# A hybrid encoder layer on one core: the first rows normalised and turned by halves, two feature tiles instead of one as plain products, splits and loads started at other places, and 32 small products of ones at the start

## The reference

```python
x = x + 0.5 * (silu(rms(x) @ w_gate1) * (rms(x) @ w_up1)) @ w_down1      # width 2816
P = rms(x) @ w_in                                                        # 7 x 512 columns
aq, ak, av, hq, hf, hi, hg = split(P)
A = chunked attention, 8 heads x 64, rms on q and k, 9 chunks of 64 keys, bias by distance
B = gated linear recurrence, 4 heads x 128, f = lb + (1 - lb) * sigmoid(hf), rms and silu gate
x = x + concat(A, B) @ w_out
x = x + 0.5 * (silu(rms(x) @ w_gate2) * (rms(x) @ w_up2)) @ w_down2
```

## Time and profile before

| | us |
|---|---|
| median of 3 runs | 1974.71 (1974.49 to 1977.51) |
| the profiled execution, its own time | 1979.15 |
| its span, first to last instruction | 1977.6 |
| PE busy in the span | 1897.7 (96%) |
| DVE, ACT, POOL busy | 1116.0, 676.9, 440.3 |
| mean granted clock of PE | 0.984 |

### The profile page before, as it was taken

The page is one execution under the profiler, slowest core; times in us unless marked ns, Lnnn a source line. Parts: engine busy times, 40 slices in busy tenths (PEclk is TensorE's granted clock), DMA queues, the critical chain, the costliest instruction groups (busy, mean ns, idle before and its releaser), DMA issues.

```text
span 1977.6 us, 24542 instructions
## 1 busy us (share of the span) xinstructions
PE 1897.7 (96%) x9296; PEld 1570.5 (79%) x9296; DVE 1116.0 (56%) x1503; ACT 676.9 (34%) x1023; POOL 440.3 (22%) x350
## 2 busy tenths in 40 slices
PE   6899999999999999999998789989999999999998
PEld 5788888887888888888887567777888888878887
DVE  6866666665555630244545664348666666655564
ACT  7333333323333432211122563244333223323332
POOL 3322422431111100011223420001422422321030
PEclk9999999999999999999998999999999999999999
DMA  5454444537755343321342410114354444468663
GB/s 163 144 183 148 159 169 146 175 135 283 247 193 195 107 155 112 117 96 64 127 142 90 144 57 1 64 64 149 139 179 146 165 162 152 149 226 284 216 195 132
DMA packets 209004, 295.50 MB, mean 149 GB/s; under 512 B 14512, under 2 KB 104760, under 8 KB 208896
## 3 DMA queue, kind: packets, MB, share of 16 engines
q1 hardware_dynamic: 193184, 253.28, 37.5%
q0 software_dynamic: 7360, 25.51, 4.0%
q10 hardware_dynamic: 8352, 15.27, 2.1%
HBM read 205.37 MB, written 91.25 MB: 150 GB/s over the span
## 4 chain that ended last, share of the span: by engine, by line
PE 89%; DVE 5%; issue 2%; ACT 2%; DMA 1%; POOL 1%; DVEq 0%; SPq 0%; ACTq 0%; POOLq 0%
PE ps L636 27%; PE ps L638 27%; PE ps L637 27%; PE ps L809 2%; PE ps L670 1%; PE ps L905 1%; PE ps L892 1%; PE ps L925 1%; DVE wlo L1494 1%; DVE hXlo L1465 0%; DVE xs L1447 0%; DMA tok_scratch<-y 0%; DVE hTlo L1425 0%; DMA xs<-x 0%; PE ps L800 0%
## 5 line engine op out<-in xcount | busy, mean ns | idle before, releaser
L636 PE MATMUL ps<-hThi,whi 128*128 128x512 f32 x864 | 338.7, 392 | 11.9 <-DVE wlo L1494 6.4
L637 PE MATMUL ps<-hTlo,whi 128*128 128x512 f32 x864 | 337.6, 391 | 0.0
L638 PE MATMUL ps<-hThi,wlo 128*128 128x512 f32 x864 | 337.5, 391 | 0.0
L636 PE MATMUL ps<-whi 128*128 128x512 f32 x616 | 241.7, 392 | 9.2 <-DVE wlo L1568 9.2
L638 PE MATMUL ps<-whi,wlo 128*128 128x512 f32 x616 | 241.1, 391 | 0.0
L637 PE MATMUL ps<-wlo,whi 128*128 128x512 f32 x616 | 241.1, 391 | 0.0
L636 PE MATMUL ps<-hXhi,whi 128*128 128x512 f32 x504 | 197.9, 393 | 8.8 <-DVE wlo L1494 8.8
L636 PEld LDWEIGHTS ps<-hThi,whi 128*128 128x128 f32 x864 | 163.1, 189 | 46.0 <-DVE wlo L1494 6.6
L637 PE MATMUL ps<-hXlo,whi 128*128 128x512 f32 x504 | 197.3, 391 | 0.0
L638 PE MATMUL ps<-hXhi,wlo 128*128 128x512 f32 x504 | 197.3, 391 | 0.0
L638 PEld LDWEIGHTS ps<-hThi,wlo 128*128 128x128 f32 x864 | 163.0, 189 | 34.1
(11 more groups left out here) (186 smaller groups left out, 2959.7 us busy)
## 6 DMA issues: line engine op xcount, KB each, us to landing
hid_scratch<-hid SPq DMA_DIRECT2D x132, 256.0 KB, 2.6
raw<-ffn_w_gate SPq DMA_DIRECT2D x44, 512.0 KB, 3.7
raw<-ffn_w_up SPq DMA_DIRECT2D x44, 512.0 KB, 4.9
wdb<-ffn_w_down SPq DMA_DIRECT2D x44, 512.0 KB, 4.1
wd_scratch<-wdb SPq DMA_DIRECT2D x88, 256.0 KB, 4.5
raw<-hid_scratch SPq DMA_DIRECT2D x80, 256.0 KB, 2.7
rawx<-hid_scratch SPq DMA_DIRECT2D x74, 256.0 KB, 2.7
raw<-w_in SPq DMA_DIRECT2D x28, 512.0 KB, 5.2
```

Of the source, the lines that this page charges most:

```text
L636: pe.matmul(dst, ahi, bhi, start=first, stop=False, skip_group_check=onto)
L637: pe.matmul(dst, ahi, blo, start=False, stop=False, skip_group_check=onto)
L638: return pe.matmul(dst, alo, bhi, start=False, stop=last, skip_group_check=onto)
```

## The change

- Two feature tiles are plain instead of one (`NPLAIN` = 2). The written start has 16 products instead of 15, and none of them needs `t2` or `t34`; each feed-forward has 156 products instead of 155. The first four products need only the first half of the width of the first four rows.
- The first four rows are normalised, turned, split and kept by halves of 512 columns, each half in one PSUM bank (`early_norm`, `early_turn`, `early_hi_part`, `early_lo_part`, `early_keep`); the squares of rows 4 to 7 stand on ACT behind all of that.
- PE begins with 24 products of a 128x128 tile of ones, 2 more after the second row's half and 6 after the fourth's (`idle_products`). The tile is filled by POOL, and the load of its later content waits for the first product.
- Pieces 0, 1 and 2 of each down projection are split during the last feature tile (`PIECE_AFTER`) instead of behind it.
- The loads of q, k, v and bias go from POOL's queue to SP's, bias and v of the second pair earlier; the masked corners are written once into the scratch tensor of the bias by two transfers. The first scores no longer wait for `kS`: unit 1 uses banks 6 and 7, and `read_out` of the last head stands behind units 0 and 1 on DVE.
- The second half of the output weights is loaded at the head of attention; the first gate and up weights of the second feed-forward behind rows 2 and 4 of `x_scratch`, instead of ahead of row 0. The first two weights of the second feed-forward are split ahead of the last row's square.
- The last piece of all counts each of its four tiles, so that each can be taken when it is done.

```diff
-START = [(0, 0), (0, 1), (1, 0), (0, 2), (0, 3), (1, 2), (0, 4), (0, 5), (0, 6), (0, 7),
-         (1, 4), (1, 1), (1, 3), (1, 5), (1, 6)]
-PRODUCTS = START + [(e, i) for e in range(2, FT) for i in range(NPROD)]
-WEIGHTS = [(0, 0), (0, 1), (1, 0), (0, 2), (0, 3), (1, 2), (1, 4), (1, 1), (1, 3), (1, 5), (1, 6)]\
-    + [(e, i) for e in range(2, FT) for i in range(NPROD)]
+START = [(0, 0), (0, 1), (1, 0), (1, 1), (0, 2), (0, 3), (1, 2), (1, 3),
+         (0, 4), (0, 5), (1, 4), (1, 5), (0, 6), (0, 7), (1, 6), (1, 7)]
+PRODUCTS = START + [(e, i) for e in range(NPLAIN, FT) for i in range(NPROD)]
+WEIGHTS = [(0, 0), (0, 1), (1, 0), (1, 1), (0, 2), (0, 3), (1, 2), (1, 3)]\
+    + [(e, i) for e in range(NPLAIN, FT) for i in range(NPROD)]
 SEQ = len(PRODUCTS)
...
+    if n <= 16:
         return PREPARED_AFTER.get(n, [])
-    return [n + 3] if n + 3 < NW else []
+    return [n - 1] if n - 1 < NW else []
 
...
+PIECE_AFTER = [(FT - 1, 1), (FT - 1, 3), (FT - 1, 4)]
...
+            return 6 if v == 1 else 2 * ((v + 1) % 2)
 
...
+            gate_up(0, 1, ffn1_w_gate, ffn1_w_up)
             for t in range(4, TT):
                 sp.dma_start(xs[:, t, :], x[0, t * P:(t + 1) * P, :]).then_inc(x_loaded[t], 16)
-            gate_up(0, 1, ffn1_w_gate, ffn1_w_up)
...
+            load_qk(0)
+            sp.wait_ge(bias_stored, 48)
+            sp.wait_ge(proj_done, PROJ_OUTS)
+            load_bias(0)
+            load_bias(1)
+            sp.wait_ge(qk_turned, 4)
+            load_qk(1)
+            stored(7)
+            load_v(0)
+            load_v(1)
+            out_pieces(1)
...
             for t in range(TT):
                 sp.wait_ge(x_added, TT + t + 1)
                 sp.dma_start(x_d[t * P:(t + 1) * P, :], xs[:, t, :]).then_inc(x_saved[t], 16)
+                if t in (2, 4):
+                    gate_up(1, t // 2 - 1, ffn2_w_gate, ffn2_w_up)
...
-                mm.then_inc(piece_done, 1)
...
+            def idle_products(n):
+                for _ in range(n):
+                    pe.matmul(ps[:, 0:P], gn[:, :], gn[:, :], start=True, stop=True)
+            pe.wait_ge(mhalf_set, 2)
+            idle_products(24)
             pe.wait_ge(ident_loaded, 16)
             for t in range(4):
+                early_turn(t, 0)
+                if t == 1:
+                    idle_products(2)
+            idle_products(6)
+            products(0, 0, 1)
+            early_turn(0, 1)
+            early_turn(1, 1)
+            products(0, 1, 2)
+            early_turn(2, 1)
+            early_turn(3, 1)
+            for t in range(4, TT):
+                products(0, t - 2, t - 1)
                 turn_tile(R_FFN1, t)
-            products(0, 0, 1)
-            turn_tile(R_FFN1, 4)
-            turn_tile(R_FFN1, 5)
-            products(0, 1, 2)
-            turn_tile(R_FFN1, 6)
...
 
+            def early_hi_part(t, h):
+                act.wait_ge(turned if h else early_turned, t + 1)
+                act.activation(hThi[:, 4 * h:4 * h + 4, t * P:(t + 1) * P],
+                               bank(early_bank(t)).rearrange("p (k c) -> p k c", k=4), ACT.Copy)\
+                   .then_inc(hT_hi_ready if h else early_hi, 1)
...
+            weight_hi(0, 2)
+            early_hi_part(0, 1)
+            early_hi_part(1, 1)
+            weight_hi(0, 3)
+            early_keep(0, 1)
+            early_keep(1, 1)
+            early_hi_part(2, 1)
+            early_hi_part(3, 1)
+            weight_hi(0, 4)
+            early_keep(2, 1)
+            early_keep(3, 1)
+            weight_hi(0, 5)
+            for t in range(4, TT):
                 square(R_FFN1, t)
-            keep_turned(R_FFN1, 0)
-            weight_hi(0, 0)
-            keep_turned(R_FFN1, 1)
-            keep_turned(R_FFN1, 2)
-            weight_hi(0, 1)
-            keep_turned(R_FFN1, 3)
-            square(R_FFN1, 4)
-            square(R_FFN1, 5)
-            weight_hi(0, 2)
-            square(R_FFN1, 6)
...
+            def early_norm(t, h):
+                dve.wait_ge(rstd_ready, t + 1)
+                if t == 0:
+                    dve.wait_ge(gain1_loaded, 16)
+                at = slice(h * HALF, (h + 1) * HALF)
+                dve.scalar_tensor_tensor(xs[:, t, at], xs[:, t, at], rstd[:, t:t + 1], gain[:, at],
+                                         ALU.mult, ALU.mult).then_inc(y_ready if h else early_y, 1)
+            def early_lo_part(t, h):
+                if h:
...
                 before = EVACS * F + t + 1
                 if q == 0:
...
+            weight_lo(0, 2)
+            early_lo_part(0, 1)
+            early_lo_part(1, 1)
+            weight_lo(0, 3)
+            early_lo_part(2, 1)
+            early_lo_part(3, 1)
+            for t in range(4, TT):
+                weight_lo(0, t)
                 normalise(R_FFN1, t)
-            hT_lo(R_FFN1, 0)
-            weight_lo(0, 0)
-            hT_lo(R_FFN1, 1)
-            hT_lo(R_FFN1, 2)
-            weight_lo(0, 1)
...
                             nmax[:, hd, t:t + 1])
                     last.then_inc(unit_max, 1)
+                if v == 1:
+                    read_out(HH - 1)
                 if 2 <= v < NV + 2 and not by_scalar(v - 2):
...
+                    weight_lo(1, 0)
+                    weight_lo(1, 1)
                 add(8 + t, t, 1)
...
+            pool.wait_ge(prod_done, 1)
             pool.dma_start(gn[:, :], hgrn_out_norm_g[0:1, :].to_broadcast([P, P])).then_inc(gn_loaded, 16)
...
+            pool.wait_ge(bias_stored, 16)
+            corner = masked.unsqueeze(1).to_broadcast([CHUNK, AH, CHUNK])
+            pool.dma_start(bias_d[:, CHUNK:P, 0:CHUNK].rearrange("h t s -> t h s"), corner)\
+                .then_inc(bias_stored, 16)
+            pool.dma_start(bias_d[:, 0:CHUNK, BAND - CHUNK:BAND].rearrange("h t s -> t h s"), corner)\
+                .then_inc(bias_stored, 16)
```

More of the change, by code:

```diff
@@ L266, in build @@
                 hXlo = keep("hXlo", [P, 12, HALF], F32R, c2)
-                gu_q = keep("gu_q", [P, HALF], where=c2)
+                gu_q = keep("gu_q", [P, NPLAIN, HALF], where=c2)
             with ExitStack() as c2:
@@ L435, in build @@
         av_loaded = [sem(f"av_loaded{p}") for p in range(2)]
-        bias_loaded = sem("bias_loaded")
-        bias_masked = sem("bias_masked")
+        bias_loaded = [sem(f"bias_loaded{p}") for p in range(2)]
         qk_sq = sem("qk_sq")
@@ L612, in _, with out_pieces, stored, load_qk @@
             wo = w_out[0].rearrange("(q k p) c -> q p k c", p=P, k=2)
[L613 removed]
+            def out_pieces(h):
                 for q in range(4):
                     piece(P_OUT + 4 * h + q, 0, wo[q][:, :, h * HALF:(h + 1) * HALF], 2)
[L616 to L617 removed]
+            def stored(n):
+                for s in range(2):
+                    sp.wait_ge(proj_stored[s], 64 * n)
+            def load_qk(p):
+                for w in range(2):
+                    sp.dma_start((qin, kin)[w], tok[:, 2 + w, p * P:(p + 1) * P]
+                                 .rearrange("(t p) c -> p t c", p=P)).then_inc(qk_loaded[w], 16)
+            def load_bias(p):
+                sp.dma_start(bias[:, p % 2, :, :], bias_d[2 * p:2 * p + 2].rearrange("h t s -> t h s"))\
+                  .then_inc(bias_loaded[p % 2], 16)
+            def load_v(p):
+                sp.dma_start(vin[:, p % 2, :, :], tok[:, 4, p * P:(p + 1) * P]
+                             .rearrange("(t p) c -> p t c", p=P)).then_inc(av_loaded[p % 2], 16)
+            out_pieces(0)
+            stored(6)
+            sp.wait_ge(y_ready, 2 * TT)
+            sp.wait_ge(turned, 2 * TT)
+            load_qk(0)
[9 more added lines that the diff above has]
+            out_pieces(1)
+            for p in range(2, PAIRS):
+                sp.wait_ge(qk_turned, 4 * p)
+                load_qk(p)
+                sp.wait_ge(unit_out, NU * (p - 1))
+                load_bias(p)
+                load_v(p)
             for t in range(TT):
@@ L1358, in _ @@
                 split(P_OUT + 4 + q)
-            for t in range(TT):
+            for t in range(TT - 1):
                 square(R_FFN2, t)
@@ L1636, in _ @@
                 t34_lo(0, j)
-            for n in range(8, SEQ):
-                after_product(0, n)
+            phases(0)
             for n in range(NPIECE):
@@ L1854, in _ @@
                 normalise(R_FFN2, t)
-            t1_lo(1, 0)
-            for w in range(4):
+            for w in range(2, 6):
                 weight_lo(1, w)
@@ L1859, in _ @@
             t1(1, 2)
-            t1_lo(1, 1)
-            weight_lo(1, 4)
-            t1_lo(1, 2)
+            weight_lo(1, 6)
+            weight_lo(1, 7)
             hT_lo(R_FFN2, 7)
             t1(1, 3)
-            weight_lo(1, 5)
-            weight_sums(1, 1)
-            t1_lo(1, 3)
-            weight_lo(1, 6)
+            for j in range(4):
+                t1_lo(1, j)
             for j in range(4):
@@ L1877, in _ @@
                 t34_lo(1, j)
-            for n in range(8, SEQ):
```

(2 more changed lines are left out.)

431 lines of the change are left out of this document (231 added, 200 removed).

## The result

| | before | changed |
|---|---|---|
| median, us (4 runs each, one chip) | 1975.99 (1974.49 to 1977.51) | 1951.81 (1946.10 to 1952.53) |
| ratio, 95% interval | | 0.9867 (0.9846 to 0.9888) |
| profiled execution: own time, span | 1979.15, 1977.6 | 1952.53, 1951.0 |

The change is faster, by 24 us (26.6 between the two profiled executions), against 42 predicted from the profiled execution. 1933 was forecast; 1951.8 lies above the range of 1921 to 1945.

A forecast was written before the change was run, and what follows sets the result against it. PE bounds the kernel, busy 1897.7 of 1977.6 us, so only its idle times and the slow clock behind them can be won. Terms sum to 42.0: 1979.15 profiled becomes 1937.1, less 4.4 to the median: 1933, range 1921 to 1945.

The forecast's parts named there:

- The start: First feed-forward's start: first product at 17.0 instead of 22.40, the 13th product's wait of 6.52 gone; 6.4 us saved.
- second feed-forward's first turns and first product: First turn's wait of 2.70 and its slow clock go, 4.2 us; first product at 1324.9 instead of 1328.34, 3.4.
- The wait of 2.25: Second feed-forward, called its twelfth product: this idle time and 1.8 us of slow clock behind it go.
- Early pieces: Down projections: splitting pieces 0 to 2 within the last tile removes PE's 4.60 idle; 6.75 us first, 6.4 second.
- Attention: 9.5 us at its head, plus 2.5 inside, where POOL's root for the next pair starts earlier.
- The head: Head of attention: scores wait for kT instead of `kS`, q of the next pair loads earlier; 9.5 us saved.
- The ones: Products of ones on PE at the start: they cost nothing and the first product runs at full clock.
- Rival 3: Six later products are no cover: DVE and ACT carry the chain to t34, waits return; 12.7, so 1946; chance 0.05.
- Rivals 1 and 4 and 5: Head of attention and start give half, 1943, 0.15; weight split loses its lead, slower, 0.03; clock holds everywhere, 1926, 0.10.
- rival 2: Clock swings in sparse stretches: first product and scores of units 2 and 3 slow, 3.6 us, 1937; chance 0.10.
- the second start: Second feed-forward's first product earlier and wait of 2.25 with its clock gone, less one extra product; 4.7 us saved.

## Why the prediction was wrong

The gain between the two profiled executions, by landmarks of PE's rows, beside the terms:

| stretch | forecast | measured |
|---|---|---|
| start, to the last product of the first feed-forward (458.97, 461.59) | 6.4 | -2.6 |
| first down projection, to the first values normalised behind it (667.31, 664.46) | 6.75 | 5.5 |
| to attention's last values (1213.25, 1196.30) | 12.0 | 14.1 |
| to the second feed-forward's first product (1328.34, 1303.49) | 7.6 | 7.9 |
| to the last matmul (1972.12, 1947.38) | 7.7 | -0.1 |
| behind it | 1.6 | 1.9 |

The forecasts of the last three rows are its terms cut at the same places: 4.2 + 3.4; 2.25 + 1.8 - 2.73 + 6.4; 1.6.

- **The start failed at one sentence**: "The wait of 6.52 is gone, because it was for the sums t3 and t4". Up to there it held: first product at 17.41 (17.0 forecast) at full clock, 3.28 of idle time before row 4's turn (3.6), the half clock behind it, the 13th product at 60.5 by counting seven products back from 79.63 (60.7), `t34` ready at 66.3 (65). But the wait was not for the sums in the kernel before either: they were complete at 60.33, 0.9 us before PE stopped. It was for the addition `gu_u`, then behind nine instructions of DVE, one of them of 1.75 us, and now behind seven, three of them stretched. The prediction took the condition that the change relaxes for the one that ended the wait. The profile's bracket names the weights' line, which is neither. 6.57 + 2.1 of half clock make 8.7 of the 9.0 us missing. Had the old 6.52 + 2.1 been kept in the sum, the term would have been -2.2; -2.6 was measured.
- **The second feed-forward's first turns and first product** were right (idle 2.85, 3.0 forecast). **The wait of 2.25** there (the prediction calls it the twelfth product's; it is the 13th's, (1,3), as at the start) was for the same addition and came back as 4.85 at the 20th, by the same order: 4.85 + 2.1, 7.0 of 7.8 missing. It grew because three operations of DVE, not one, ran beside POOL's sums; with POOL held back it is 1.59. The first product's own half clock, which the forecast had, is not in this.
- **Early pieces** were right in their mechanism and somewhat high: 4.60 went twice, the first stretch gained 5.5 of 6.75, and undoing them cost 11.3 us where 13.15 stood. 0.96 came back at 479.03, at the seventh piece; ACT had waited 3.04 us for its load and DVE made its low part right behind. No run tested that.
- **Attention** was right in its mechanism, and low by 2 in sum, which hides two errors that cancel. The head gave 7.5 of the 9.5: the turn of unit 2 came at 1084.33 where 1094.71 stood, less the 2.85 won before, with the first scores at 1071.57 as forecast and those of units 2 and 3 still at half clock. From there to the last values 6.6 came where 2.5 was forecast: the borders of pairs are at 1.53 instead of 2.44 and 2.51, and the half clock is gone at 1137 and at the end (0.87 and 0.79 in those stretches before, 1.00 now).
- **The ones** cost nothing, as forecast, and gave the first product its clock.
- **Rivals.** Rival 3 had the waits come back and their price, 1946, but blamed the sums `t3` and `t4` and got 0.05. It is the nearest to what happened; the argument against it, that the sums are ready in time, was right and beside the point. Rivals 1 and 4 and 5 did not occur: there is no idle time from 100 to 455. Of rival 2, the scores are at half clock and the first product is not.

Two terms fell, 6.4 and the 4.7 of the second start: a wait counts as gone only when the condition that ended it has been named from the trace. With them at -2.6 and about -2, 42 becomes 26, the measured change. That the rest fits so well is in part luck: attention gave 2.1 more, the first pieces 1.3 less.

A rule on DVE and POOL bears on the stretch. The rows show that only DVE's operations with both inputs in SBUF take up to 1.78 us beside POOL's sums, those that read PSUM 0.68. The Trainium skill's page "SBUF — State Buffer", section "Who interferes with whom", says that a DVE instruction with two SBUF inputs contends with a GpSimd instruction that reads SBUF, and that the ports they share are an exclusive lock. The trace agrees on which operations are stretched. It agrees with the lock in the main: beside each other, one operation of each engine passes per 1.7 us, a little less than the 0.68 and 1.26 that they take alone, one after the other.

## What to carry to other kernels

Before you call a wait gone, list every semaphore of the waiting instruction from the code, and find in the trace when the producer of each ended. The one that ended about 0.1 us before the engine went on is the cause; one that ended before the engine stopped is not, even if it is the one your change relaxes. A bracket can name a neighbour of the producer. Then do the same for the instruction at the new place, and price each producer by what stands ahead of it in its engine's queue, at the durations beside the neighbours it will then have. An engine's or a queue's place in line is a cost of its own: the store that mattered here was 256 KB, ready 6.5 us before it was issued. Behind a removed wait there is often a second one that it hid, here of about its size; remove one, look again, and move a producer rather than holding back an engine whose later work others need.
